# A decoder step with 32 experts: from the fifth expert on, the experts run in an order by their block counts, heavy and light by turns

## What is computed

```python
logits = xt @ w_router + b_router            # 264 tokens, 32 experts
top_val, top_idx = lax.top_k(logits, TOP_K)  # TOP_K = 4
gates = jax.nn.softmax(top_val, axis=-1)
...
def _clamped_swiglu(xb, wgu, bgu, wd, bd):
    gu = xb @ wgu + bgu                      # 1024 -> 2048
    glu, lin = gu[:, :D_FF], gu[:, D_FF:]
    glu = jnp.minimum(glu, SWIGLU_LIMIT)
    lin = jnp.clip(lin, -SWIGLU_LIMIT, SWIGLU_LIMIT)
    return ((lin + 1.0) * glu * jax.nn.sigmoid(SWIGLU_ALPHA * glu)) @ wd + bd   # 1024 -> 1024
...
y = jax.ops.segment_sum(y_buf[dest] * gate_sorted[:, None], tok_sorted, num_segments=T)
```

## Time and profile before

| | |
|---|---|
| timed runs | 1259.64, 1260.22, 1266.55 us; median 1260.22 us |
| span of the profiled execution | 1258.5 us |
| TensorE (PE) busy | 1102.0 us, 88% of the span |
| VectorE (DVE) busy | 588.2 us, 47% |
| ScalarE (ACT) busy | 230.7 us, 18% |
| GpSimd (POOL) busy | 68.5 us, 5% |
| read from HBM | 479.47 MB, 385 GB/s over the span with what is written |

### The profile page before, as it was taken

How to read it: one execution, slowest core, us unless ns; L and a number is a source line. 1 busy time by engine, 2 the same in 40 slices (tenths; PEclk the granted TensorE clock), 3 DMA queues, 4 the chain that set the end, 5 groups by cost and what they waited for, 6 DMA issues and landing times.

```text
span 1258.5 us, 23992 instructions
## 1 busy us (share of the span) xinstructions
PE 1102.0 (88%) x9856; PEld 456.6 (36%) x9856; DVE 588.2 (47%) x1166; ACT 230.7 (18%) x420; POOL 68.5 (5%) x126
## 2 busy tenths in 40 slices
PE   8999999999988697996887979999966995667996
PEld 4776777785322131321222322333211331112332
DVE  3536744444654252563353544666532552332654
ACT  3002510141311110220111211112100211100212
POOL 0312020250100000000000000000000000000000
PEclk9999999999989897998798999999988998888999
DMA  9979994599899999999999999999999999999995
GB/s 342 312 245 347 317 339 154 187 384 366 284 428 429 426 429 426 429 425 429 426 428 428 428 426 393 409 424 427 428 427 428 427 426 430 424 431 425 428 428 236
DMA packets 67619, 485.30 MB, mean 386 GB/s; under 512 B 6421, under 2 KB 29450, under 8 KB 40762
## 3 DMA queue, kind: packets, MB, share of 16 engines
q1 hardware_dynamic: 59312, 461.07, 88.9%
q0 software_dynamic: 7104, 19.65, 4.9%
q10 hardware_dynamic: 1130, 3.51, 0.8%
HBM read 479.47 MB, written 4.72 MB: 385 GB/s over the span
## 4 chain that ended last, share of the span: by engine, by line
DMA 45%; PE 27%; DVE 1%; issue 0%; DVEq 0%; ACT 0%; ACTq 0%
DMA big<-in_w_down 26%; PE PB L1247 13%; DMA big<-in_w_gate_up 13%; PE PB L1274 7%; DMA hTG<-in_w_down 5%; PE PB L1214 2%; PE PB L1201 2%; PE PB L1206 1%; PE PB L1229 1%; PE PB L1221 1%; PE PB L1240 0%; PE PB L1186 0%; PE PB L1232 0%; DVE big L1623 0%; DVE big L1620 0%
## 5 line engine op out<-in xcount | busy, mean ns | idle before, releaser
L1247 PE MATMUL PB<-big,cst 128*32 128x512 f32 x2768 | 355.0, 657 | 109.2 <-DMA big<-in_w_gate_up 109.2
L2189 DVE TENSOR_TENSOR tok<-PB,cst 32x512 f32<-32x512 f32 x188 | 129.1, 687 | 261.7 <-ACT cst L1554 259.8
L1247 PEld LDWEIGHTS PB<-big,cst 128*32 128x32 f32 x2768 | 89.0, 115 | 345.2 <-issue 181.1
L1274 PE MATMUL PB<-big,cst 128*32 128x512 f32 x1408 | 166.6, 602 | 12.8 <-DMA big<-in_w_down 12.7
L2165 DVE TENSOR_SCALAR mod<-PB 64x256 f32<-64x256 f32 x96 | 41.0, 427 | 209.1 <-PE PB L1247 208.4
L756 PE MATMUL PB<-hTG,big 128*128 128x264 f32 x576 | 136.5, 391 | 0.4 <-DVE hTG L1617 0.4
L756 PEld LDWEIGHTS PB<-hTG,big 128*128 128x128 f32 x576 | 106.9, 190 | 27.3 <-issue 10.8
L1544 ACT ACTIVATE mod<-PB 64x256 f32<-64x256 f32 x96 | 36.1, 376 | 422.3 <-PE PB L1247 421.7
L1274 PEld LDWEIGHTS PB<-big,cst 128*32 128x32 f32 x1408 | 39.2, 110 | 96.8 <-issue 65.8
L1201 PE MATMUL PB<-wide,att 128*32 128x256 f32 x784 | 57.9, 415 | 5.1 <-DVE att L2159 4.9
L1554 ACT ACTIVATE cst<-PB 128x512 f32<-128x512 f32 x48 | 28.7, 597 | 178.2 <-PE PB L1274 178.2
(11 more groups left out here) (378 smaller groups left out, 970.9 us busy)
## 6 DMA issues: line engine op xcount, KB each, us to landing
big<-in_w_gate_up SPq DMA_DIRECT2D x115, 2048.0 KB, 31.0
big<-in_w_down SPq DMA_DIRECT2D x57, 2048.0 KB, 23.9
hTG<-in_w_gate_up SPq DMA_DIRECT2D x13, 2048.0 KB, 37.1
big<-in_w_mod SPq DMA_DIRECT2D x24, 1024.0 KB, 7.5
big<-in_w_in SPq DMA_DIRECT2D x22, 1024.0 KB, 9.2
hTG<-in_w_down SPq DMA_DIRECT2D x6, 2048.0 KB, 24.0
wide<-in_cache_k POOLq DMA_DIRECT2D x16, 256.0 KB, 6.8
big<-in_w_out SPq DMA_DIRECT2D x4, 1024.0 KB, 10.5
```

Of the source, the lines that this page charges most:

```text
L1247: mm = pe.matmul(GU[32 * j:32 * j + 32, :], mo["xT"][:, (2 * u + r) * M:(2 * u + r + 1) * M], groups(w[:, r * 2 * D:(r + 1) * 2 * D])[:, j ...
L1274: mm = pe.matmul(DN[32 * j:32 * j + 32, :], mo["actT"][:, (4 * u + r) * M:(4 * u + r + 1) * M], w[:, r * D + half * 512:r * D + (half + 1) ...
L2189: mm = dve.tensor_tensor(mo["y"][rows, :], DN[rows, :], mo["y_part"][other, :], ALU.add)
```

## The change

The experts 0 to 3 stay in their places (FIXED = 4). For the other 28, VectorE computes an order while the chip runs. Each expert gets a key, 64 times its blocks less its number, and its rank is the number of keys above its own; the first four get keys above all others. So rank 4 goes to the expert with the most blocks, and among equals to the lower number. A constant row `ranks` says which rank runs at which place: 0, 1, 2, 3, and then 4, 31, 5, 30, and so on to 17, 18. From it come the table `order` (which expert runs at a place), new values of `tab` and `used_tab`, the bias selector `sel`, and new slots for all tokens (`places`, `grel`). The loads take the expert's number from `order`, so that their addresses come from a register. SyncE waits for `order_ready` before unit 24, the first of place 4, and TensorE before place 4.

```diff
+FIXED = 4
...
+    heavy = np.arange(FIXED, (E + FIXED) // 2)
+    pairs = np.stack([heavy, E - 1 + FIXED - heavy], 1).reshape(-1)
+    put("ranks", np.tile(np.concatenate([np.arange(FIXED), pairs]), (P, 1)))
...
             for n in range(NSLOT, NLOAD):
                 e, u = (n - NSLOT) // NU, (n - NSLOT) % NU
+                if e == FIXED and u == 0:
+                    sp.wait_ge(S("order_ready"), 1)
...
+                if n // NU >= FIXED and n % NU == 0:
+                    if n // NU == FIXED:
+                        sp.wait_ge(S("order_ready"), 1)
+                    expert = sp.value_load(order[0:1, n // NU:n // NU + 1], min_val=0, max_val=E - 1)
                 sp.wait_ge(S("w_used"), before + (u + 1))
-                if n < NLOAD - 1:
+                if n < FIXED * NU:
                     load_unit(n)
+                elif n < NLOAD - 1:
+                    load_unit(n, expert)
...
+                if e == FIXED:
+                    pe.wait_ge(S("order_ready"), 1)
...
-            with dve.Fori(0, before_last) as b:
-                expert_block(b)
+            def block_sums(b):
                 dve.wait_ge(S("y_copied"), b + 1)
...
+            def order_experts():
...
+                stt(keys, sv("nb"), 2.0 * E, iota_e, ALU.mult, ALU.subtract)
+                ts(keys[:, 0:FIXED], iota_e[:, 0:FIXED], -1.0, 32.0 * E, ALU.mult, ALU.add)
+                do(dve.transpose(key_of, keys))
+                ts(ahead, keys, key_of[:, 0:1], None, ALU.is_gt)
+                do(dve.tensor_reduce(col[0], ahead, AX, ALU.add))
+                ts(at_place, C("ranks"), col[0], None, ALU.is_equal)
...
+                copy(order[0:1, :], turned[0:1, :])
...
+                copy(tab[0:1, FIXED + 1:E], sv("incl", FIXED, E - 1, rows=1))
+                ts(used_tab[0:1, FIXED:E], sv("incl", FIXED, E, rows=33, r0=32), -1.0, float(NU), ALU.add, ALU.mult)
+                copy(sel[:, FIXED:E], at_place[0:96, FIXED:E])
+                dve.nop().then_inc(S("order_ready"), 1)
...
+                tt(places, sv("cmp").unsqueeze(1).to_broadcast([P, NCH, E]), places, ALU.add)
...
+                do(dve.tensor_reduce(sv("grel"), picked.rearrange("p c k e -> p (c k) e"), AX, ALU.add))
...
+            expert_block(0)
+            order_experts()
+            block_sums(0)
+            with dve.Fori(1, before_last) as b:
+                expert_block(b)
+                block_sums(b)
```

More of the change, by code:

```diff
@@ L59 @@
                 ("steps", 9), ("slot", 1), ("causal", 128), ("bias", H * 384), ("scan", T),
-                ("sbias", PAST + 1), ("pair", 32), ("selt", NS), ("maps", 2), ("lamc", 2), ("valid", 2)]
+                ("sbias", PAST + 1), ("pair", 32), ("selt", NS), ("maps", 2), ("lamc", 2), ("valid", 2), ("ranks", E)]
 CONST = {}
@@ L199, in build @@
                             for i in range(4))
-        tab = sb("tab", [1, E + 2], I32)
-        used_tab = sb("used_tab", [1, E], I32)
+        tables = sb("tables", [33, E + 2], I32)
+        tab, used_tab = tables[0:1, :], tables[32:33, 0:E]
+        order = sb("order", [1, E], I32)
         pgt = sb("pgt", [1, NS * NPG], I32)
@@ L402, in _, with unit_rows, load_unit @@
             win = a["w_in"][0].rearrange("(k p) n -> p k n", p=P)
-            def load_unit(n):
-                e, u = n // NU, n % NU
+            def unit_rows(n, e):
+                u = n % NU
                 if u < 4:
-                    src = a["w_gate_up"][0, e, u * 2 * P:(u + 1) * 2 * P, :].rearrange("(p r) n -> p (r n)", r=2)
-                else:
-                    src = a["w_down"][0, e, (u - 4) * 4 * P:(u - 3) * 4 * P, :].rearrange("(p r) n -> p (r n)", r=4)
+                    return a["w_gate_up"][0, e, u * 2 * P:(u + 1) * 2 * P, :].rearrange("a (p r) n -> p (a r n)", r=2)
+                return a["w_down"][0, e, (u - 4) * 4 * P:(u - 3) * 4 * P, :].rearrange("a (p r) n -> p (a r n)", r=4)
+            def load_unit(n, e=None):
+                src = unit_rows(n, slice(n // NU, n // NU + 1) if e is None else bass.ds(e, 1))
                 sp.dma_start(unit_slot(n), src).then_inc(unit_landed(n)[0], 16)
@@ L479, in _ @@
                 e, u = (n - NSLOT) // NU, (n - NSLOT) % NU
+                if e == FIXED and u == 0:
+                    sp.wait_ge(S("order_ready"), 1)
                 if n == NSLOT or u == 0:
                     before = sp.value_load(used_tab[0:1, e:e + 1], min_val=0, max_val=NU * MAXB)
+                if n // NU >= FIXED and n % NU == 0:
+                    if n // NU == FIXED:
+                        sp.wait_ge(S("order_ready"), 1)
+                    expert = sp.value_load(order[0:1, n // NU:n // NU + 1], min_val=0, max_val=E - 1)
                 sp.wait_ge(S("w_used"), before + (u + 1))
-                if n < NLOAD - 1:
+                if n < FIXED * NU:
                     load_unit(n)
+                elif n < NLOAD - 1:
+                    load_unit(n, expert)
                 else:
-                    src = a["w_down"][0, E - 1, 4 * P:8 * P, :].rearrange("(p r) n -> p (r n)", r=4)
+                    src = unit_rows(n, bass.ds(expert, 1))
                     for i, (r0, r1) in enumerate(LAST_ROWS):
@@ L2124, in _ @@
             ts(tab[0:1, E + 1:E + 2], sv("incl", E - 1, E, rows=1), -1.0, None, ALU.add)
-            ts(used_tab[0:1, :], sv("incl", rows=1), -1.0, float(NU), ALU.add, ALU.mult)
+            ts(used_tab[0:1, :], sv("incl", rows=33, r0=32), -1.0, float(NU), ALU.add, ALU.mult)
             dve.nop().then_inc(S("tab_ready"), 1)
@@ L2190, in _, with total, as_row @@
                 mm.then_inc(S("y_ready"), 1)
+            def order_experts():
+                keys, key_of, ahead, at_place = (sv(n) for n in ("vaT", "vbT", "osa", "osb"))
+                lgf = lg.rearrange("p c e -> p (c e)")
+                spots, turned, weighed = (lgf[:, E * i:E * (i + 1)] for i in range(3))
+                col = [sv("l", i, i + 1) for i in range(5)]
+                iota_e = C("iota_e")
+                def total(at, of):
+                    tt(weighed, at, of, ALU.mult)
+                    do(dve.tensor_reduce(at_col, weighed, AX, ALU.add))
+                def as_row(row, of):
+                    copy(spots, of.to_broadcast([P, E]))
+                    do(dve.transpose(row, spots))
+                stt(keys, sv("nb"), 2.0 * E, iota_e, ALU.mult, ALU.subtract)
[4 more added lines that the diff above has]
+                ts(at_place, C("ranks"), col[0], None, ALU.is_equal)
+                at_expert = keys
+                do(dve.transpose(at_expert, at_place))
+                at_col = col[1]
+                total(at_expert, iota_e)
+                as_row(turned, col[1])
+                copy(order[0:1, :], turned[0:1, :])
+                at_col = col[2]
+                total(at_expert, sv("nb"))
+                as_row(turned, col[2])
+                do(dve.tensor_tensor_scan(sv("incl"), C("ones")[:, 0:E], turned, 0.0, ALU.mult, ALU.add))
+                copy(tab[0:1, FIXED + 1:E], sv("incl", FIXED, E - 1, rows=1))
+                ts(used_tab[0:1, FIXED:E], sv("incl", FIXED, E, rows=33, r0=32), -1.0, float(NU), ALU.add, ALU.mult)
+                copy(sel[:, FIXED:E], at_place[0:96, FIXED:E])
+                dve.nop().then_inc(S("order_ready"), 1)
+                at_col = col[3]
+                total(at_place, iota_e)
+                as_row(turned, col[3])
+                stt(weighed, turned, col[3], sv("nb"), ALU.is_lt, ALU.mult)
+                do(dve.tensor_reduce(col[4], weighed, AX, ALU.add))
+                as_row(sv("cmp"), col[4])
+                ts(sv("cmp"), sv("cmp"), -1.0, float(M), ALU.add, ALU.mult)
+                tt(places, sv("cmp").unsqueeze(1).to_broadcast([P, NCH, E]), places, ALU.add)
+                choices = sv("idf").rearrange("p (c k) -> p c k", c=NCH)[:, :, 0:TOPK]
+                for c in range(NCH):
+                    tt(picked[:, c, :, :], iota_e.unsqueeze(1).to_broadcast([P, TOPK, E]),
+                       choices[:, c, :].unsqueeze(2).to_broadcast([P, TOPK, E]), ALU.is_equal)
+                    tt(picked[:, c, :, :], picked[:, c, :, :],
+                       places[:, c, :].unsqueeze(1).to_broadcast([P, TOPK, E]), ALU.mult)
+                do(dve.tensor_reduce(sv("grel"), picked.rearrange("p c k e -> p (c k) e"), AX, ALU.add))
+                ts(sv("grel", 2 * TOPK, 3 * TOPK), sv("grel", 2 * TOPK, 3 * TOPK), C("valid")[:, 1:2], None, ALU.add)
```

## The result

The changed kernel takes 1276.47 us (median of 4 runs, 1273.84 to 1279.66) against 1260.03 us (median of 4, 1259.64 to 1266.55). The ratio is 1.0109, with a 95% interval of 1.0079 to 1.0139: slower by 0.8 to 1.4%. The profiled execution took 1273.84 us with a span of 1272.1 us, 13.6 us more than the span before.

A forecast was written before the change was run, and what follows sets the result against it. The expert stage was taken as bound by its weight loads. Terms 0 - 0 + 14.5 = +14.5 us, all from the last place's second block, took the median from 1260.22 to 1274.7 us, range 1268.5 to 1280.

The forecast's parts named there:

- The loads bound the stage, and the last place pays for its blocks: End of expert stage: loads set the pace, and the last place's second block adds 14.5 us with nothing left to load.
- The order of places from the block counts: Expert places: 15 heavy experts for 14 heavy turns, so the last place gets a two-block expert where it had one block.
- one heavy expert less: Rival, last place has a one-block expert through a miscount: not slower, 1260.2 us, or 1256.1 with the hole closed; chance 0.06.
- The hole moves and stays: Loads of the three-block expert: the 4.1 us hole in DMA rate moves from 784 to some 460 us; gain 0.
- The rival in which the hole closes: Middle of the expert stage: the hole closes while the end grows, 14.5 - 4.1, so 1270.6 us; chance 0.14.
- The order's 38 instructions hidden: VectorE after block 0's transpose: order computed in 9.8 us, TensorE waits 2 us in block 1, cost 0.
- the queue's slack: Load issued at 372.45, its transfer reckoned to begin about 392.8, 20 us later, so a 2 us delay vanishes.
- the upper bound of 22.4 us: Order computation: all 38 instructions at 0.59 us make TensorE 14.6 us late and still leave 5 us.
- Register-addressed loads free: Expert weight loads: register addresses and 28 more table loads on SyncE cost 0, bounds 0 to 0.54 us per load, hidden.
- The lower clock in the added block: Rival, last place's added block: at the lower clock it takes 24.1 us instead of 14.5, 1284 us; chance 0.03.

The follow-up runs named there:

- experiment 1: Changed kernel with places 29 and 31 exchanged in the row of ranks, so a one-block expert is last: 1265.03 us, ratio to before 1.0014.
- experiment 3: Experts by number with the computed order's machinery kept, last two exchanged so a two-block expert is last: 1273.71 us, ratio to before 1.0105.
- experiment 4: Changed kernel with places 4 and 31 exchanged, so the three-block expert 15 is last: 1290.54 us, ratio to before 1.0222.
- experiment 6: Changed kernel with 120 more VectorE instructions inside the computation of the order: 1301.86 us, ratio to before 1.0326.
- experiment 2: Changed kernel with the experts run in order of their numbers, all order machinery kept: 1260.17 us, ratio to before 1.0000.
- experiment 8: Experts by number, machinery kept, with experts 27 and 30 exchanged so both last places have one block: 1264.32 us, ratio to before 1.0010.
- experiment 5: Changed kernel with 40 more VectorE instructions inside the computation of the order: 1274.64 us, ratio to before 1.0106.

## Why the prediction was right

1. **The loads bound the stage, and the last place pays for its blocks.** Right, and the whole of the result. By its own steps place 30 was to end its first block at 1216.34 and 1230.85 its second, the last place at 1245.35 and after 14.51 us more; the profile shows 1215.37, 1229.88, 1244.38 and 1258.89. The weights end at 1244, 28 us before the end where 30 were foretold. Experiments 1 and 3 isolate it from both sides: 14.3 us taken away, 14.2 us put in.
2. **The order of places from the block counts.** Right: 48 blocks, a two-block expert last. Had there been one heavy expert less, the last place would have had one block, and experiment 1 shows that the kernel would then have been no slower.
3. **The hole moves and stays.** Right: from 785 to 460 us. Its price of 4.1 us was mis-sized, however, and so was its length in the new place, about 4 us against 2.3. It was read from the mean rate of all DMA engines, and experiment 4 shows what its removal is worth to the stage, 1.6 us. In the sum this did no harm, since it stood on both sides. The rival in which the hole closes, at 1270.6 us, should have stood at 1273.1, 2.5 us higher, where a time can't tell it from the forecast. For interleaving there was nothing to join but the three-block expert: in both stretches of the earlier trace rows the loads bind the stage, at 427 GB/s, and only TensorE's share differs.
4. **The order's 38 instructions hidden.** Right: 9.9 us against 9.8, TensorE waits 2.5 us and is 1.8 us late by the stage's clock (367.67 - 336.9 against 366.50 - 337.6), where 2 were reckoned, and nothing of it shows in the stage. The bound behind it was off: the queue's slack is 15 us, not 20. The sum took the start of the load's transfer from TensorE's use of the unit, 397.74 less one unit's 4.90, which is 392.8; experiment 6 shows the queue dry at 390.4, 2.4 us before that. It left out the 1.7 us from the issue of a load to its data (414.81 to 416.5 in experiment 6, counted at 428 GB/s), and the load itself goes out 1.2 us later in the changed kernel (373.65 against 372.45): 20.4 - 2.4 - 1.7 - 1.2 = 15.1. At the upper bound of 22.4 us, 14.6 of them late, it would just have been enough.
5. **Register-addressed loads free.** Right, by experiment 2.
6. **The lower clock in the added block.** It doesn't come: 14.50 us, granted clock 1.00 from 1240 to 1260 us. The low clock does show in a starved last block: 0.60 from 1235 to 1240 us in experiment 8.
7. The median is 1.8 us above the forecast; the other two kernels of the same stage length have 1273.71 and 1274.64. The stage itself is 0.3 us shorter than forecast, so the difference lies in front of it, most likely in TensorE's first 30 us (last section); of the four executions only the profiled one can be looked into.

## What to carry to other kernels

In these runs work behind the last byte of the weights was paid in full (14.2 us of stage for one block more, of 14.5 us), and work elsewhere was free as long as the queue of loads didn't run dry (experiments 5 and 6: 907.8 us against 907.5 with 40 more instructions, 934.4 with 120 more). So where a stream of weights is the bound, an order should first be judged by what stands last (in a table cut into pairs of heavy and light, both members of the middle pair may be heavy). Before interleaving heavy and light stages, compute whether the bound resource ever idles; here it did so for 1.6 us in 900.

## What the runs showed of the hardware

A hole in the mean rate of the DMA engines overstated its price here: 4.1 us of missing rate were worth 1.6 us and 2.3 were worth 1.3, and the same kind of stall measured 2.3, 4.1 and 5.1 us at 460, 785 and 937 us.

The spread of the times comes from TensorE's first 30 us. Two executions, first the kernel by number, then that with the three-block expert at place 20, whose program is the same up to the expert stage. TensorE, 16 small matmuls of one kind and then the start of the first long group, and the load queue near the first of the projection weights:

```profile
16.66 1.07 PE L690 MATMUL PB<-big 128*32 128x256 f32 x16
23.31 7.36 PE L772 MATMUL PB<-hTG,big 128*128 128x264 f32 x32 [0.41 <-DVE hTG L1635]
```

```profile
52.80 0.37 SPq L455 DMA_DIRECT2D big<-in_w_in  x1
```

```profile
18.80 1.93 PE L692 MATMUL PB<-big 128*32 128x256 f32 x16
29.05 7.78 PE L774 MATMUL PB<-hTG,big 128*128 128x264 f32 x32
```

```profile
58.97 0.37 SPq L457 DMA_DIRECT2D big<-in_w_in  x1
```

Both executions begin with TensorE at about half its later speed, 1.93 us for such 16 matmuls. In the first they take 1.07 us from 13.55 us on, in the second they still take 1.94 at 23.95 us. So the long group starts 5.7 us later, the load that waits for its slot goes out 6.2 us later, and the expert stage starts at 342.8 instead of 336.4. The time is never made up. In all ten profiled executions the two go together: the long group starts between 22.96 and 29.05 us and the stage between 336.4 and 342.8, in nearly the same order, with 336.5 for the first and 342.8 for the last. The granted clock in the profile reads 1.00 from 13 to 30 us in both, so it does not show the slow phase; only the durations do. Why it lasts longer in some executions, no run here shows.
